# A hybrid decoder layer on one core: the attention gate projected in two passes by token half, with query and key stacks and first scores beside the second

## What is computed

```python
xn = rms_norm(h, pre_norm[i])
proj = xn @ w_in[i]                       # ... n_q, keys and values, branch gates, n_z
o_gla = rms_norm(o_gla, gla_out_norm[i]).reshape(B, T, GLA_WIDTH)
o_gla = (o_gla * jax.nn.silu(g_z)).astype(x.dtype)
# in nsa_mixer, for each block of 128 queries and each of the three branches:
s = jnp.einsum('bqhgd,bkhd->bhgqk', qblk, kw)
p_win = jax.nn.softmax(jnp.where(mw, s, -1e30), axis=-1)
o_win = jnp.einsum('bhgqk,bkhd->bqhgd', p_win, vw)
o = g[..., 0:1] * o_cmp + g[..., 1:2] * o_slc + g[..., 2:3] * o_win
o_nsa = (o_nsa * jax.nn.silu(n_z)).astype(x.dtype)
mixed = jnp.concatenate([o_gla, o_nsa], axis=-1) @ w_out[i]
```

## Time and profile before

| what | value |
|---|---|
| time, median of 3 runs | 922.89 us (922.48 to 926.85) |
| the profiled execution's own time | 924.57 us |
| its span, first to last instruction | 922.5 us |
| mean granted clock of TensorE in it | 0.973 |
| DMA over the span | 46.48 MB read from HBM, 4.19 MB written |

### The profile page before, as it was taken

One profiled execution on the slowest core, in us unless ns is written; L12 is line 12 of the kernel. 1 busy time (PEld: TensorE's weight loads), 2 busy tenths in 40 slices (PEclk: granted clock), 3 DMA queues, 4 the chain that ended last, 5 costly groups with the idle time before them and its releaser, 6 DMA issues.

```text
span 922.5 us, 12594 instructions
## 1 busy us (share of the span) xinstructions
PE 852.4 (92%) x4674; PEld 704.8 (76%) x4674; DVE 513.1 (56%) x1061; ACT 461.0 (50%) x1011; POOL 369.2 (40%) x309
## 2 busy tenths in 40 slices
PE   2999999999999999975999999999999999999993
PEld 2787798888888788855677777777867888887882
DVE  5301349281652602067799998999976035364426
ACT  5311343312232015427898888899976252625432
POOL 1212015416132122460654744555544446463554
PEclk9999979999999999997799999999999999999997
DMA  6342011102111010000000000000006723232342
GB/s 222 89 97 48 12 43 38 54 24 51 31 46 47 24 45 23 24 1 21 1 1 1 1 1 1 1 1 1 1 1 231 247 81 103 81 102 71 99 162 103
DMA packets 36524, 51.48 MB, mean 56 GB/s; under 512 B 11104, under 2 KB 17520, under 8 KB 36464
## 3 DMA queue, kind: packets, MB, share of 16 engines
q1 hardware_dynamic: 36464, 50.69, 18.1%
HBM read 46.48 MB, written 4.19 MB: 55 GB/s over the span
## 4 chain that ended last, share of the span: by engine, by line
PE 73%; DVE 14%; ACT 6%; issue 3%; POOL 3%; DMA 1%; SPq 0%; POOLq 0%; DVEq 0%; ACTq 0%
PE psum L643 51%; DVE pT_lo L1582 4%; PE psum L839 3%; PE psum L730 3%; PE psum L854 3%; PE psum L825 2%; PE psum L826 2%; DVE p_win L1559 2%; PE psum L855 2%; PE psum L687 2%; DVE p_slc L1559 1%; DVE o_sum L1592 1%; ACT pT_hi L1122 1%; ACT qT_hi_lo L1100 1%; ACT p_win L1113 1%
## 5 line engine op out<-in xcount | busy, mean ns | idle before, releaser
L1225 POOL TENSOR_TENSOR w_lo<-w_raw,w_hi 128x512 fp32r<-128x512 f32 (+1 forms) x128 | 175.5, 1373 | 374.8 <-ACT w_hi L942 374.3
L942 ACT ACTIVATE w_hi<-w_raw 128x512 fp32r<-128x512 f32 (+1 forms) x128 | 79.5, 625 | 330.4 <-PE psum L643 310.2
L1582 DVE TENSOR_TENSOR pT_lo<-psum,pT_hi 128x512 fp32r<-128x512 f32 (+1 forms) x148 | 100.6, 685 | 7.5 <-ACT pT_hi L1122 6.8
L643 PE MATMUL psum<-w_hi,xT_hi 128*128 128x512 f32 x256 | 101.2, 395 | 1.7 <-DVE gla_state_b L1511 1.7
L643 PE MATMUL psum<-w_lo,xT_hi 128*128 128x512 f32 x256 | 100.4, 392 | 0.0
L643 PE MATMUL psum<-w_hi,xT_lo 128*128 128x512 f32 x256 | 100.3, 392 | 0.0
L1122 ACT ACTIVATE pT_hi<-psum 128x512 fp32r<-128x512 f32 (+1 forms) x148 | 87.2, 591 | 23.4 <-PE psum L839 22.3
L1259 POOL TENSOR_SCALAR p_slc<-p_slc,gate_over_sum 128x640 f32<-128x640 f32 (+7 forms) x32 | 57.4, 1804 | 60.7 <-DVE gate_over_sum L1568 60.7
L825 PE MATMUL psum<-kT_hi_hi,qT_hi_lo 128*128 128x512 f32 (+3 forms) x192 | 72.0, 380 | 1.5 <-DVE neg_max L1559 1.2
L854 PE MATMUL psum<-pT_hi,v_hi_lo 128*128 128x512 f32 x132 | 61.3, 464 | 12.0 <-DVE pT_lo L1582 10.0
L643 PE MATMUL psum<-xT_hi,w_hi 128*128 128x512 f32 x176 | 69.0, 392 | 0.1
(11 more groups left out here) (231 smaller groups left out, 1943.0 us busy)
## 6 DMA issues: line engine op xcount, KB each, us to landing
w_raw<-in_w_in SPq DMA_DIRECT2D x48, 256.0 KB, 2.7
w_raw<-in_w_out SPq DMA_DIRECT2D x32, 256.0 KB, 2.7
w_raw<-in_ple_gate SPq DMA_DIRECT2D x32, 256.0 KB, 2.5
...
```

Source lines behind the costliest of these rows:

```text
L643: mm = pe.matmul(out, lhs, rhs, start=(first and n == 0), stop=(final and n == 2))
L942: act.activation(Wh[:, i % SPLIT, 0:w], raw[:, i % RAW, 0:w], ACT.Copy).then_inc(s_whi, 1)
L1225: pool.tensor_tensor(Wl[:, i % SPLIT, 0:w], raw[:, i % RAW, 0:w], Wh[:, i % SPLIT, 0:w].bitcast(F32), ALU.subtract).then_inc(s_wlo, 1)
L1582: dve.tensor_tensor(PTl[0:n, u % 4], bank(4 + u % TRING)[0:n], PTh[0:n, u % 4].bitcast(F32), ALU.subtract).then_inc(s_plo, 1)
```

## The change

1. The chunk nz is split by token half: nzA projects tokens 0 to 511 into banks 1, 3, 0, 2 and nzB the other half into banks 1, 3, 6, 7. Each takes all eight pieces of the weights, which are loaded and split once for each pass. A piece has 12 matmuls in each pass.
2. The pieces of nzB, its sigmoids and products, and the stacks become operations of `attention_timeline`, which places them among the attention's own. In a stack's place in memory, query half 0 covers only the part of xT_hi that nzB doesn't read. The stacks are reordered: four query stacks of half 0, the compressed one, four key stacks of half 0, then half 1. The first nine may come before the end of nzB; the rest, and every `turn` and `values`, come after its last piece.
3. `qorder` now depends on the key head: 3, 2, 1, 0, 4, 5, 6, 7 for the first, 7, 0, 6, 1, 5, 2, 4, 3 for the second. In the first four tiles the window's scores lie in the upper half of the selected branch's buffer, since p_win's place is still in use.
4. The gain is multiplied in by VectorE, right after gz has been read. GpSimd takes GLA's inverse roots in two groups of four tiles between splits of nzA.
5. The masks are loaded after the fifth piece of nzB and the fourth stack.

```diff
-            ("nz", True, KD, 8, 512),
+            ("nzA", True, KD, 4, 512), ("nzB", True, KD, 4, 512),
...
-    qorder = [t for i in reversed(range(NT // 2)) for t in (NT - 1 - i, i)]
+    qorder = ((3, 2, 1, 0, 4, 5, 6, 7), (7, 0, 6, 1, 5, 2, 4, 3))
+    EARLY = 4
...
+    stacks = [("q", h, 0) for h in range(4)] + [("c", 0, 0)] + [("k", h, 0) for h in (0, 2, 1, 3)] \
+        + [(kind, h, 1) for hs in ((0, 1), (2, 3)) for kind in "qk" for h in (hs if kind == "q" else (hs[0] // 2, hs[0] // 2 + 2))]
+    first_half = 9
+    stack_bank = [4, 5, 0, 2, 4, 5, 4, 5, 4] + [1, 3] * 4
...
+    gate_bank = {"nzA": (1, 3, 0, 2), "nzB": (1, 3, 6, 7)}
...
+    def buffer_free(s):
...
+        late = EARLY <= s // 3 < EARLY + 2 and s % 3 == 1
+        return first_unit[s - 5 + late]
...
+        for k in range(KD):
+            if k >= 2:
+                ops["gate_hi", k] = "A", 640, 5
+                after["gate_hi", k] = [("gate_mm", k - 3)]
+                ops["gate_lo", k] = "G", 1380, 0
+                after["gate_lo", k] = [("gate_hi", k)]
+            ops["gate_mm", k] = "P", 2720, 5
+            after["gate_mm", k] = [("gate_lo", k)]
...
+        if br == 2 and s // 3 < EARLY:
+            return PSL[:, (s // 3) % 2, :, 512:1024]
...
-        wait_chunk_read(pe, cidx["nz"])
-        for u in range(len(stacks)):
+        project("nzA", xt, lambda b: pe.wait_ge(s_oge, gate_bank["nzA"][b] + 1))
+
+        def gate_piece(k):
+
+            c = cidx["nzB"]
+            i = piece0[c] + k
+            pe.wait_ge(s_wlo, i + 1)
...
+                pe.matmul(out, wh[:, cols], XTh[:, k, 512:1024], start=(k == 0), stop=False)
+                pe.matmul(out, wh[:, cols], XTl[:, k, 512:1024], start=False, stop=False)
+                mm = pe.matmul(out, wl[:, cols], XTh[:, k, 512:1024], start=False, stop=(k == KD - 1))
...
+            if chunks[c][0] == "nzA" and k in (5, 7):
+                half = (k - 5) // 2
+                pool.wait_ge(s_og, 4 * half + 4)
+                ts = slice(4 * GH * half, 4 * GH * half + 4 * GH)
+                inverse_rms(GSS[:, 1, ts], GSS[:, 2, ts], GSS[:, 0, ts], GDV, 4 * GH, s_orms)
...
+        gate_gla(0)
+        read_out(cidx["nzA"])
+        gate_gla(1)
```

More of the change, by code:

```diff
@@ L433, in scaled_count, with stacks_needed @@
         return sum(scaler[br].count(e) for _, _, br in steps[:s + 1])
+    stacks = [("q", h, 0) for h in range(4)] + [("c", 0, 0)] + [("k", h, 0) for h in (0, 2, 1, 3)] \
[4 more added lines that the diff above has]
+    def buffer_free(s):
+        if s < 6:
+            return 0
+        late = EARLY <= s // 3 < EARLY + 2 and s % 3 == 1
+        return first_unit[s - 5 + late]
+    def stacks_needed(step):
+        kv, qt, br = step
+        if qt >= NT // 2:
+            return len(stacks)
+        last = [("q", 2 * kv + 1, 0), ("c", 0, 0) if br == 0 else ("k", (br - 1) * NKV + kv, 0)]
+        return max(stacks.index(x) for x in last) + 1
     def attention_timeline():
         ops, after = {}, {}
+        for k in range(KD):
[6 more added lines that the diff above has]
+            after["gate_mm", k] = [("gate_lo", k)]
+        for b in range(4):
+            ops["gate_sig", b] = "A", 560, 0
+            after["gate_sig", b] = [("gate_mm", KD - 1), ("gate_mul", b - 2)]
+            ops["gate_mul", b] = "V", 690, 0
+            after["gate_mul", b] = [("gate_sig", b)]
+        for u, (kind, _, half) in enumerate(stacks):
+            before = [v for v in range(u) if stack_bank[v] == stack_bank[u]]
+            ops["stack_turn", u] = "P", {"q": 450, "k": 1130, "c": 450}[kind], 0
+            after["stack_turn", u] = [("stack_lo", v) for v in before[-1:]] \
+                + [("gate_mm", KD - 1), ("gate_mul", u % 2)] * half
+            ops["stack_hi", u] = "A", {"q": 1220, "k": 500, "c": 280}[kind], 0
+            after["stack_hi", u] = [("stack_turn", u)]
+            ops["stack_lo", u] = "V", {"q": 1420, "k": 600, "c": 280}[kind], 0
+            after["stack_lo", u] = [("stack_hi", u)]
         for s, step in enumerate(steps):
@@ L444, in attention_timeline @@
                 ops["score", n] = "P", 0.83 * nk + 60, s
-                after["score", n] = [("mask_max", n - 2)]
+                after["score", n] = [("mask_max", n - 2), ("stack_lo", stacks_needed(step) - 1)]
                 ops["mask_max", n] = "V", 1.04 * nk + 120, s
-                after["mask_max", n] = [("score", n), ("turn", first_unit[s - 5] - 1 if s >= 6 else -1)]
+                after["mask_max", n] = [("score", n), ("turn", buffer_free(s) - 1)]
                 ops["exponent", n] = "A", 0.83 * nk + 250, s
@@ L464, in attention_timeline @@
             ops["values", u] = "P", 430, s
-            after["values", u] = [("low", u), ("output", j - ORING)]
+            after["values", u] = [("low", u), ("output", j - ORING), ("gate_mul", 3)]
         for j in range(2 * NT):
@@ L471, in attention_timeline @@
         kinds = ["values", "half", "output", "low", "high", "turn", "gate", "scaleV", "scaleA", "scaleP",
-                 "exponent", "mask_max", "score"]
+                 "exponent", "mask_max", "score", "gate_mul", "gate_sig", "stack_lo", "stack_hi", "stack_turn",
+                 "gate_lo", "gate_hi", "gate_mm"]
         queue = {k: sorted(n for kind, n in ops if kind == k) for k in kinds}
-        free, end, line = {"P": 0, "V": 0, "A": 0, "G": 0}, {}, []
+        free, end, line = {"P": 0, "V": 7000, "A": 3000, "G": 0}, {}, []
         while len(line) < len(ops):
@@ L498, in build_program @@
     scaled = {"V": s_normd, "A": s_norma, "P": s_norm}
-    stacks = [("k", h, half) for h in range(4) for half in range(2)] + [("c", 0, 0)] \
-        + [("q", h, half) for h in range(4) for half in range(2)]
     def probs(s):
         kv, qt, br = steps[s]
+        if br == 2 and s // 3 < EARLY:
+            return PSL[:, (s // 3) % 2, :, 512:1024]
         return (PCM, PSL, PWN)[br][:, (s // 3) % 2]
@@ L836, in turn @@
                 pe.wait_ge(s_plo, u - TRING + 1)
+            else:
+                pe.wait_ge(s_qlo, first_half)
             n = min(P, span(qt, br)[1])
@@ L1236, in _ @@
                    ("nq", 3): 6}
-        for i in range(piece0[cidx["nz"]] + 2):
+        for i in range(piece0[cidx["nzB"]] + 2):
             split_lo(i)
```

174 lines of the change are left out of this document (115 added, 59 removed).

## The result

The changed kernel takes 918.85 us (median of 5 runs, 915.7 to 919.4), the kernel before in the same job 923.83 us (5 runs, 922.48 to 926.85). The ratio is 0.9938, with a 95% interval of 0.9916 to 0.9959: a gain of 0.6%, 5 us, where 13.5 were forecast. The profiled execution took 917.71 us, with a span of 915.9 and a mean granted clock of 0.980.

What follows compares the result with a forecast made beforehand. TensorE and VectorE were each left free in adjoining stretches, to be overlaid; VectorE priced the loop. Gate end 421.3, loop 241.7, tail 19.2, extras 1.3 gave 683.5 against 697.0: 13.5 us less, 909.4 us, range 898 to 918.5.

Steps and rivals of the forecast that it cites:

- The first pass: Gate projection nzA on TensorE: 96 matmuls of 0.228 us, from 363.23 to 385.1 us.
- the second: Gate projection nzB on TensorE: starts at 387.6 us, after four query stacks and 0.7 us of waits for banks.
- The first score: Start of attention scores on TensorE, among the second pass's pieces: expected near 398.5 us, against 436.71 before.
- The two more table loads: ScalarE, sigmoids between exponentials: two more loads of 1.28 us; 1.3 us taken with score-buffer waits, bounds 0 to 4.
- VectorE's work left: VectorE after the gate's end at 421.3 us: 236.5 us of attention, half stacks and gate products still to do.
- The tail: After the last score: 13 units instead of 9, so 17 us become 19.2, 2.2 more.
- at the body's share 225.3/0.932 = 241.7: Attention loop: VectorE's 225.3 us without the tail, at its earlier busy share 0.932, take 241.7 us, to 663.0.
- No real overlap: Rival: early scores wait until the second pass has ended; 8 to 9 us lost, 918 us; chance 0.07.
- Fuller loop: Rival: VectorE always has a score waiting in the attention loop, share 0.97; 9.4 us less, 900.0 us; chance 0.12.
- ScalarE in the small tiles: Rival: fixed order holds ScalarE at 0.80 in first head's tiles 3 to 0; 60 us, not 51.5; 917.9 us; chance 0.10.
- its sign: Sign of a wrong forecast: VectorE under 0.90 from 421 to 475 us with ScalarE over 0.93.
- Half clock: Rival: TensorE's clock stays at half in the small tiles' block; 24.5 us more, 933.9 us; chance 0.07.

Runs made afterwards that it cites:

- run 1: Kernel before with only its query tiles put in the changed kernel's order, no second pass or early scores: 930.77 us against 924.28, ratio 1.008.
- 6: Kernel before with gain and norms moved and the changed kernel's tile order, gate in one pass: 926.7 us, ratio 1.003.
- 4: Kernel before with only the gain on VectorE and GpSimd's inverse roots in two groups, one gate pass, old order: 917.18 us, ratio 0.9928.
- run 5: Changed kernel, planned so the first score comes after the last gate matmul; second pass and early stacks stay: 924.79 us, ratio 1.0013.
- run 9: Changed kernel with one list of both heads' tiles, small tiles last, and planner durations nearer the measured ones: 906.25 us, ratio 0.9812.
- run 10: Changed kernel with the first head's tiles as 3 0 2 1 4 5 6 7, nothing else: 914.26 us, ratio 0.9897.
- run 12: Changed kernel with the tile list of run 9, but planned with the changed kernel's own durations: 911.64 us, ratio 0.9851.

## Why the prediction was wrong

The forecast was 909.4 us, with 918.5 as its upper end; the kernel took 918.85.

**What held.** Up to 422 us the sum ran as told. The first pass ended at 386.0 (385.1 forecast; half of the difference is that it began at 363.73), and the second, behind four query stacks, began at 388.6 (387.6): TensorE waited 0.59 us for banks of nzA (0.7) and 0.53 ahead of the first key stack (1). The first score came at 399.12 (398.5) and the gate ended at 422.0 (421.3). A key stack took 1.03 to 1.09 us and not 0.89; on four of them that is half a microsecond. There was no wait for w_lo there and the clock was 1.00. The two more table loads came too. VectorE's work left was 228.1 + 10.0 = 238.1 us (236.5). The tail came out near its price, though I had read it loosely: the 17 us of the earlier trace rows begin before the last scores and end 1.1 us behind the first transpose of gla_z. The last score and that transpose before, and the last score with the change:

```profile
682.03 0.27 PE L826 MATMUL psum<-kT_lo_lo,qT_hi_lo 128*128 128x128 f32 x1
...
695.91 3.65 PE L872 MATMUL psum<-consts,gla_z 128*128 128x128 f32 x32
```

```profile
669.28 0.40 PE L900 MATMUL psum<-kT_lo_lo,qT_hi_lo 128*128 128x512 f32 x1
```

With the transpose at 688.94 (in the rows of the result) that is 13.9 and 19.7 us, 5.8 more for four more units, where the sum has 5.1 (2.9 of them inside the body). The two rows of the table that meet at 673 put the first 3.7 us of this tail into the body.

**What failed** is one step: "at the body's share 225.3/0.932 = 241.7". From 422 to 673 VectorE was busy for 228.1 of 251 us, a share of 0.909; up to the last score it was 224.5 of 247.3, 0.908. At 0.932 these 224.5 us would have taken 240.9, and the 6.4 us between are as much as the forecast missed on the trace's clock, where gla_z came 7.0 us earlier and not 13.5. The bounds had been read from two windows of the old order, 0.951 and 0.914, and they were not its limits: its row from 460 to 500 us, shown at run 1, has 38.70/40 = 0.968, so "in no window" was wrong too. The new order's whole body lies below both. A share is a property of an order with its plan, and the change replaced both. I gave the new order a price of 2.2 us in the tail and one rival, and none in the sum of the body. Runs 1 and 6 measure it: 6.5 us in the kernel before, 9.5 with the norms moved. In the traces of 4 and 6, 9.0 us apart behind the gate, 5.8 of that are the tail and 3.2 the loop up to the last score, which should have become 2.9 shorter, since four units had left it. No run has the old order of both heads beside the second pass, so there its price is carried over from these two. The parts of the forecast without it, norms and overlap, are −7.1 and −7.9 us, 15.0 together, where I had forecast 13.5 + 2.2 = 15.7: that part of the mechanism was right.

**The other rivals.** "No real overlap" fell with run 5. "Fuller loop" asked for 0.97 and got 0.908; even run 9 has 0.931. "ScalarE in the small tiles" had the place right and the engine wrong, and that the time, 918.85, lies by its 917.9 is luck. Of its sign only half came: from 421 to 475 us VectorE was at 46.45/54 = 0.86, but ScalarE at 46.71/54 = 0.87 and not over 0.93. I had read 48 us of ScalarE's work against 48 of VectorE's and put a price on ScalarE. In the first place, 460 to 500 us, neither is full: VectorE 34.35, ScalarE 33.61, TensorE 34.83 of 40. With tiles 1 and 0 side by side the steps have one or two units each, so each engine would wait for the chain of the others. That is an argument from the list; run 10 shows that the place fills when they are not neighbours (36.22 of 40), in a kernel 4.6 us faster, with the reservation made there.

**The second place** I had not seen at all. In the changed kernel, from 576.7 to 582.2 us, VectorE's timeline has only units, and three of the four wait for ScalarE's pT_hi:

```profile
576.69 0.69 DVE L1698 TENSOR_TENSOR pT_lo<-psum,pT_hi 128x512 fp32r<-128x512 f32 x1
579.01 0.69 DVE L1698 TENSOR_TENSOR pT_lo<-psum,pT_hi 128x512 fp32r<-128x512 f32 x1 [1.62 <-ACT pT_hi L1216]
579.90 0.69 DVE L1698 TENSOR_TENSOR pT_lo<-psum,pT_hi 128x512 fp32r<-128x512 f32 x1 [0.20 <-ACT pT_hi L1216]
581.59 0.69 DVE L1698 TENSOR_TENSOR pT_lo<-psum,pT_hi 128x512 fp32r<-128x512 f32 x1 [1.00 <-ACT pT_hi L1216]
582.20 1.08 DVE L1675 CUSTOM_DVE_ANT_0 p_slc<-psum,masks 128x896 f32<-128x896 f32 x1
```

A unit by itself comes every 1.28 us and keeps VectorE busy for 0.69 of them; masks have to fill the rest. With large tiles in a row the masks of the next one are done early, and those of the one after find no free p_slc buffer until tile 7 is turned. I had used the pitch of 1.28 for the tail, and it holds wherever masks run out. That the buffer alone makes the hole is argued, not shown: run 12 against run 9 shows that with the same list and buffers the plan can fill it.

**Half clock** I had as a matter of the whole block or nothing. It came as two short spells at the first place, 1.5 and 3 us behind a wait for a mask. The table of stretches for TensorE, and the two waits on its timeline:

```profile
468.00:470.00 2.00, 1.50 (x11) 0.97 0.00 0
470.00:472.00 2.00, 2.00 (x9) 0.50 0.00 0
472.00:474.00 2.00, 2.00 (x10) 0.68 0.00 0
...
484.00:486.00 2.00, 2.00 (x9) 0.50 0.04 8
486.00:488.00 2.00, 2.00 (x13) 0.77 0.01 4
```

```profile
468.37 0.30 PE L899 MATMUL psum<-kcT_hi_hi,qT_hi_lo 128*128 128x64 f32 x1 [0.93 <-DVE neg_max L1675]
...
480.28 0.50 PE L899 MATMUL psum<-kT_hi_hi,qT_hi_lo 128*128 128x512 f32 x1 [1.24 <-DVE neg_max L1675]
```

By the clocks of these stretches and of 482 to 484 (0.88) they are some 6.8 us at half clock in all, which can cost at most half of that, 3.4 us; how the 4 us of the place divide between them and the empty chain stays open. The rule that I had cited (the Trainium skill, "TensorE: Matmul & The Clock Gate", section "A second HAM failure mode: psum-queue depth-cycling") thus had its case here in a small form, though the tail, with a wait of 0.49 us behind every second unit, again stayed at 1.00.
